# Down product: weight pairs that slide through five places, with the gate multiplied into the weight rows

## What is computed

```python
def conv_ffn(h, conv_state, w_up, w_conv, b_conv, w_down):
    ...
    a, g = jnp.split(uc, 2, axis=-1)
    out = (jax.nn.silu(a) * g) @ w_down          # (2048 x 2816) @ (2816 x 1024)
    ...
    x = x + g2 * f_out                           # g2: 1024 values, the same for every prompt token
```

## Time and profile before

| what | us |
| --- | --- |
| median of three runs | 3072.58 (3071.22 to 3073.42) |
| the profiled execution | 3067.53, its span 3065.9 |
| PE busy in the span | 2902.4 (95%) |
| DVE, ACT, POOL busy | 1959.0, 1265.5, 775.3 |
| down product, first to last matmul | 2507.2 to 3060.4 |

### The profile page before, as it was taken

How to read it: one execution, slowest core, us unless ns; L and a number is a source line. 1 busy time by engine, 2 the same in 40 slices (tenths; PEclk the granted TensorE clock), 3 DMA queues, 4 the chain that set the end, 5 groups by cost and what they waited for, 6 DMA issues and landing times.

```text
span 3065.9 us, 49134 instructions
## 1 busy us (share of the span) xinstructions
PE 2902.4 (95%) x17179; PEld 2518.6 (82%) x17179; DVE 1959.0 (64%) x2943; ACT 1265.5 (41%) x2510; POOL 775.3 (25%) x678
## 2 busy tenths in 40 slices
PE   7999999999999999999989999999999988779799
PEld 5878888887778888888879999999999976557577
DVE  2300016624988999786677777777777786676765
ACT  4611112224777887445553333334232232232322
POOL 3310003313666776120110000000000033343432
PEclk8999999999999999999999999999999999989899
DMA  6322224534422440886644444445566655535344
GB/s 215 111 77 76 74 74 153 159 123 114 125 57 58 90 95 11 304 290 197 211 170 162 155 152 154 152 148 189 179 216 210 203 182 181 193 120 198 110 151 143
DMA packets 339306, 458.54 MB, mean 150 GB/s; under 512 B 68194, under 2 KB 219944, under 8 KB 336454
## 3 DMA queue, kind: packets, MB, share of 16 engines
q1 hardware_dynamic: 325608, 415.96, 42.8%
q0 software_dynamic: 12208, 40.46, 4.0%
q10 hardware_dynamic: 1332, 0.06, 0.0%
HBM read 284.90 MB, written 171.48 MB: 149 GB/s over the span
## 4 chain that ended last, share of the span: by engine, by line
PE 44%; issue 6%; DVE 4%; POOL 3%; DMA 3%; ACT 1%; SPq 0%; DVEq 0%; POOLq 0%; ACTq 0%
PE facc L2907 29%; PE eacc L2886 6%; PE dacc L2907 4%; POOL dres L1867 2%; DMA x_d<-dres 1%; PE mpT L3056 1%; DMA dpart<-act_d 1%; PE mpm L3065 1%; PE mpS L3075 1%; PE eyT L2869 0%; POOL dT_plain L1870 0%; PE mpT L3106 0%; PE mpN L3091 0%; PE exT L2899 0%; PE mpN L3095 0%
## 5 line engine op out<-in xcount | busy, mean ns | idle before, releaser
L767 PE MATMUL pacc<-pring,h1H 128*128 128x512 f32 x1360 | 431.4, 394 | 3.4 <-ACT h1H L326 3.4
L2907 PE MATMUL facc<-fright,fsums 128*128 128x416 f32 x2112 | 418.1, 353 | 9.9 <-ACT facc L2018 6.9
L2907 PEld LDWEIGHTS facc<-fright,fsums 128*128 128x128 f32 x2112 | 398.3, 189 | 15.7 <-issue 7.5
L1183 POOL TENSOR_TENSOR aS<-aS,aC 128x512 f32<-128x512 f32 (+3 forms) x326 | 334.6, 1034 | 152.1 <-DVE aC L1123 145.7
L1123 DVE TENSOR_TENSOR_SCAN aC<-aB,aC,a 128x512 f32<-128x512 f32 (+3 forms) x326 | 362.8, 1113 | 12.1 <-ACT aB L1079 1.1
L767 PEld LDWEIGHTS pacc<-pring,h1H 128*128 128x128 f32 x1360 | 256.5, 189 | 56.4 <-ACT h1H L326 3.5
L2907 PE MATMUL facc<-fright,fwH 128*128 128x416 f32 x1056 | 290.5, 356 | 12.8 <-DVE fU L2451 11.0
L767 PE MATMUL pacc<-pring,h1L 128*128 128x512 f32 x640 | 248.0, 389 | 0.0
L1867 POOL TENSOR_TENSOR dres<-dres,dy 128x512 f32<-128x512 f32 x86 | 149.9, 1743 | 303.3 <-DVE dy L2581 234.2
L1870 POOL TENSOR_TENSOR dT_plain<-dT_plain,dB_plain 128x512 f32<-128x512 f32 x2 | 2.5, 1287 | 867.9 <-DMA db_third<-w_down 867.9
L2907 PEld LDWEIGHTS facc<-fright,fwH 128*128 128x128 f32 x1056 | 200.5, 191 | 17.7 <-issue 12.5
(11 more groups left out here) (382 smaller groups left out, 5942.4 us busy)
## 6 DMA issues: line engine op xcount, KB each, us to landing
sums_d<-fsums SPq DMA_DIRECT2D x88, 512.0 KB, 2.9
fsums<-sums_d SPq DMA_DIRECT2D x88, 512.0 KB, 4.8
fraw<-w_up SPq DMA_DIRECT2D x66, 512.0 KB, 4.1
proj_out<-pstage SPq DMA_DIRECT2D x119, 256.0 KB, 2.0
dres<-x_d SPq DMA_DIRECT2D x92, 256.0 KB, 3.3
qk_T<-pturn POOLq DMA_DIRECT2D x68, 256.0 KB, 3.1
mwa<-w_ada SPq DMA_DIRECT2D x16, 1024.0 KB, 6.6
dpart<-act_d SPq DMA_DIRECT2D x32, 512.0 KB, 4.7
```

The source lines that it names most:

```text
L767: op = mm_(acc[:, n % NB], h[:, kk, tok(t)], weight(q, w), start=(j == 0), stop=(j == len(order) - 1))
L1183: nc.gpsimd.tensor_tensor(at, at, buf[:, a + 1:b + 1], ALU.mult).then_inc(w_ready, 1)
L2907: mm = nc.tensor.matmul(bank, a[:, kk], b[:, kk], start=(begins and kk == 0 and m == 0), stop=(kk == count - 1 and m == 2), skip_group_che ...
```

## The change

Nothing ahead of the down product is changed, nor is the number of its matmuls. In it:

- **Weights slide.** There are five places for pairs. Pair 3 comes in at unit 2, pair 4 at unit 4, and so on; each stays for eight units (`STAY`). Pairs 0 and 1 leave early, at units 4 and 6, and come again at units 20 and 22. A unit works on `WINDOW[w]`: three pairs in units 0, 1 and 18 to 23, four in units 2 to 17.
- **Cells of a coming pair** are made inside the two units before it is used: its two rows are loaded (512 KB each), the sample's product runs on them at the head of the even unit, POOL multiplies them by the gate (`gate_row`), DVE makes the four sums in the even unit and the seven low halves in the odd one, ACT three of the high halves in the even unit and four in the odd one.
- **Outputs.** With the gate in the weights, DVE adds P5 to the residual (`add_five`, twice a unit) and then the bank (`add_out`, four times). `take_five`, `add_residual`, `finish_out`, `dy` and `dP` are gone.
- **Activations** come as halves into three places; the first half of unit w + 2 waits for the lefts of unit w, the second for those of w + 1.
- **First group.** POOL multiplies B11, B12 and B21 and makes T1; DVE multiplies B22 and makes T2, T4, T3 and all seven low halves.

The diff, cut:

```diff
-    GROUPS = ((0, 3), (6, 4), (14, 4))
+    NK = NF // 2
+    FIRST, ACTIVE, PLACES = 3, 4, 5
+    STAY = [(0, 4), (0, 6), (0, 8)] + [(2 * n - 4, 2 * n + 4) for n in range(FIRST, NK)] + [(20, UNITS), (22, UNITS)]
+    WINDOW = [[n for n, (a, b) in enumerate(STAY) if a <= w < b] for w in range(UNITS)]
+    COMING = {2 * v: n for v, n in enumerate([*range(FIRST, NK), None, NK, NK + 1])}
...
+            def load_act(w, e):
+                if w >= 2:
+                    sp.wait_ge(left_low, 7 if w == 2 else 7 * (w - 1 + e))
...
+            def load_rows(v):
...
+                    sp.wait_ge(*low_of("B22", COMING[2 * v - 2]))
                 for a in range(2):
+                    sp.dma_start(raw_rows[:, a], d["w_down"][(2 * kp + a) * P:(2 * kp + a + 1) * P, :]).then_inc(raw_rows_in, 16)
...
             for w in range(UNITS):
                 if w == 1:
                     store_narrow(NF - 1)
+                    sp.wait_ge(act_stored, (WIDE_STORES + NARROW_STORES) * NF)
...
+                if w + 2 < UNITS:
+                    load_act(w + 2, 0)
                 store_out(w, 0)
+                if w + 1 in COMING and w > 0:
+                    load_rows((w + 1) // 2)
                 store_out(w, 1)
...
+                if w == 1:
+                    sp.wait_ge(ends_taken, 1)
+                    for t in range(2):
+                        sp.dma_start(d["conv_out"][t], ends_t[:, t]).then_inc(ends_stored, 16)
+                    sp.wait_ge(ends_stored, 32)
+                if w + 1 < UNITS:
+                    load_res(w + 1, 2)
                 if w + 2 < UNITS:
-                    load_act(w + 2)
+                    load_act(w + 2, 1)
                 store_out(w, 3)
...
-            def add_residual(w, j):
+            def gate_row(a, n):
+                pool.wait_ge(down_gate_in, 48)
+                pool.wait_ge(raw_rows_in, 48 * event(n) + 48)
+                pool.wait_ge(sample_done, event(n) + 1)
+                nc.gpsimd.tensor_tensor(raw_rows[:, a], raw_rows[:, a], down_gate[:], ALU.mult).then_inc(cell_gated, 1)
+            def first_blocks():
...
+                for blocks_, half in ((first, 0), (b12_rows, 1), (b21_rows, 0)):
+                    for n in range(FIRST):
+                        op = nc.gpsimd.tensor_tensor(blocks_[n], blocks_[n], first_gate[half], ALU.mult)
...
-                    v.tensor_tensor(y_, down_a if j == 0 else down_b, gate_, ALU.mult).then_inc(down_gated, 1)
+            def add_five(w, j):
+                dve.wait_ge(done["P5"], UP + w + 1)
+                dve.wait_ge(res_in[j], 16 * w + 16)
+                v.tensor_tensor(res_of(w, j), res_of(w, j), down_e, ALU.add).then_inc(five_added, 1)
+            def add_out(w, j):
+                dve.wait_ge(done[("P2", "P7", "P3", "P4")[j]], UP + w + 1)
...
             def down_unit(w):
+                if w in COMING and w > 0:
+                    sample_down(w // 2)
                 for name in PRODUCTS:
...
-                        pe.wait_ge(c22_taken, UP + w + 1)
+                        pe.wait_ge(out_ready, 4 * w + 2)
```

More of the change, by code:

```diff
@@ L1954, in _ @@
             store_h2(final)
[L1955 to L1959 removed]
+            first_blocks()
+            for n in COMING.values():
+                if n is not None:
+                    gate_row(0, n)
+                    gate_row(1, n)
         @block.scalar
@@ L2169, in down_slot @@
+                if w % 2 and coming is not None:
+                    for name in HIGHS[1][3:]:
+                        cell_high_of(name, coming)
                 down_seed_b(w)
-                if changed:
-                    cell_high_of("T3", g)
-                take_five(w)
-                if change:
-                    cell_high_of("B11", g + 1)
-                down_seed_c(w)
-                if changed:
-                    cell_high_of("B22", g)
-                if w + 1 == UNITS:
-                    return
@@ L2569, in cell_low_of, with first_low_of @@
+            def first_low_of(name):
+                dve.wait_ge(cell_high, HIGHS[0].index(name) + 1)
+                dve.wait_ge(cell_sum, {"T1": 1, "T2": 2, "B22": 3}.get(name, 0)) if name in ("T1", "T2", "B22") else None
+                if name == "B11":
+                    dve.wait_ge(cell_sum_pool, 1)
+                top, low, own = first_cells(name)
+                if name == "B21":
+                    for n in range(FIRST):
                         op = v.tensor_tensor(low[:, n], b21_rows[n], top[:, n].bitcast(F32), ALU.subtract)
@@ L3033, in down_unit @@
                     else:
-                        pe.wait_ge(c22_taken, UP + w + 1)
-                    three(banks[name], left(one, w)[0:2], cell(other, g)[0:2], name in ("P1", "P5"), done[name])
+                        pe.wait_ge(out_ready, 4 * w + 2)
+                    high, low, _ = left(one, w)
+                    for i, n in enumerate(WINDOW[w]):
+                        b_high, b_low_, _ = cell(other, n)
+                        for m, (a, b) in enumerate(((high, b_high), (high, b_low_), (low, b_high))):
+                            mm = nc.tensor.matmul(banks[name], a[:, i], b, start=(name in ("P1", "P5") and i == 0 and m == 0),
+                                                  stop=(i == len(WINDOW[w]) - 1 and m == 2), skip_group_check=True)
+                    mm.then_inc(done[name], 1)
+                    if (w, name) == (0, "P7"):
+                        sample_down(0)
                     if (w, name) == (1, "P2"):
```

529 lines of the change are left out of this document (245 added, 284 removed).

## The result

The changed kernel takes 3034.5 us (median of four runs, 3032.8 to 3039.4), the kernel before 3072.1 us beside it: ratio 0.988, 95% interval 0.9863 to 0.9897. So 37.6 us less, where 64.2 were forecast.

The account below looks back on a forecast made before the run. TensorE needs 441 of the down product's 553.2 us; 112 are idle time and half clock. Unit times summed to 489.7 (-63.5), with -0.7 at the end: 3072.6 - 64.2 = 3008.4 us; range 2980 to 3040, likeliest case 2994 to 3030.

Parts of the forecast that it names:

- the holes at units 8 and 16: TensorE stops of about 15 us at each of two weight-group changes, caused on VectorE and GpSimd; forecast to go.
- The loop: Activation load waits behind residual load, which waits for output 2's store; 41.2 us per pair of four-pair units bringing new pairs.
- Rival 2: Loop longer: 22.5 us for each of 18 units, waits adding up to 0.1 us per operation; 3049 us; chance 0.13.
- Three-pair units: Units 18 to 23: the loop gives 18.2 and 18.8 us, 74.0 for units 18 to 21; then 15.9 and 14.8.
- The entry: Units 0 and 1: VectorE gets 18.6 us more work, loses meetings with GpSimd; TensorE +7, so 54.6 us.
- GpSimd's part in the even units: Two 1024-column multiplications of 2.5 us each run while VectorE waits for activations, so they cost nothing.
- GpSimd's first blocks: Entry: twelve 512-column operations, about 16 us, hidden behind the up product; counted at 0, with 6 us kept.
- The new rows: New pair's rows land in about 5 us; TensorE waits about 1 us (0 to 3) at unit heads, seven times.
- Rival 3: Slower: GpSimd's lock costs 5 us plus 2.5 us of clock per gated pair, 11 at entry; 3095 us; chance 0.09.
- Rival 1: The loop hides: half loads land in 3.3 us, rows never late, entry +4; 2986 us; chance 0.13.
- the list of signs: No hole over 5 us; units 2 to 17 at 19.6 to 21.5, 18 to 21 at 17.5 to 19.5; GpSimd operation near 2.5.

Follow-up runs that it names:

- x1: Changed kernel with the load of the activations' second half put ahead of the residual load in SP's queue: 3015.5 us, ratio 0.9818.
- x2: Changed kernel with the activations' second half loaded, from unit 2 on, once VectorE's sum S4 is done, ahead of store 2: 3010.9 us, ratio 0.9798.
- x7: Changed kernel with GpSimd's gate multiplication of each coming weight row cut to 2 columns from 1024: 3029.6 us, ratio 0.9853.
- x4: Changed kernel with GpSimd's first gate waiting for output 2 of unit 0, and ScalarE's unit 1 copy of bank a to b before four T cells: 3031.0 us.
- x11: x9 with ScalarE's copy of bank b to c in unit 1 also moved before the four high halves of T blocks: 3000.1 us, ratio 0.9772.
- x8: Changed kernel with GpSimd's gate multiplications of the first blocks cut to 2 columns from 512: 3034.6 us, ratio 0.9873.
- y2: Kernel before, with GpSimd's additions of the residual cut to 2 columns from 512: 3045.7 us, ratio 0.9917.
- y1: Kernel before, keeping its three groups, with VectorE adding P5 and banks into the residual, no gate, no ScalarE copy of P5 or GpSimd additions: 3042.3 us, ratio 0.9897.
- x9: Changed kernel with the edits of x4 and x2, and output 1 ahead of the coming pair's last sums and low half on VectorE: 2999.8 us, ratio 0.9766.
- x3: Changed kernel with ScalarE copying bank b to c between the high halves of A11 and S1: 3039.6 us, ratio 0.9895.

## Why the prediction was right, and where it was not

**The total.** The down product came out 33.5 us over its forecast (523.2 for 489.7), which is over half of the gain that was forecast. That the total stayed in the range is in part luck: it owes as much to the range's width of 60 us as to the sum. What the prediction had right is the mechanism: the holes at units 8 and 16 go, and a loop through store and load takes part of it back (x1, x2).

**The loop** was named right, with its place and its path. Its size was off mostly in one term, the load: "4.0, since it travels alone". It did not travel alone. The residual load into place 2 was issued just ahead of it and store 3 0.4 us behind. From the first low half in unit 8 (2711.36) to that in unit 9 (2733.77) are 22.4 us: 13.2 for VectorE's 19 operations (forecast 12.8), 2.9 from the issue of the store to that of the load (2.6), 5.6 from there to ScalarE (4.0), 0.7 for ScalarE's copy (0.6). Over the fourteen such loads of units 3 to 16 it is 5.2 us on average (4.75 to 6.0) from issue to ScalarE. What makes one longer than another no run here separates: in unit 10 the load has the same neighbours in the queue and takes 4.75. The issue table of the last two visits, from issue to landing, gives 4.7, the upper bound that the earlier trace rows showed before:

```profile
dres<-x_d SPq DMA_DIRECT2D x63, 256.0 KB, 3.5
dpart<-act_d SPq DMA_DIRECT2D x17, 512.0 KB, 4.7
...
draw_rows<-w_down SPq DMA_DIRECT2D x12, 512.0 KB, 4.4
```

Rival 2, the longer loop, had 22.5 us a unit; 22.1 is the mean over units 2 to 15. So these units lie near rival 2's figure and not at the forecast's 20.7, and the whole, between the two, is nearer to rival 2 (3049) than to the forecast. But rival 2's reason is not what happened: it put a tenth of a microsecond on each operation, and the 19 operations took 0.4 us more than counted; it is the load again.

The terms as written do not quite give the sum either. What follows output 2 (2.1, 0.4, 0.1, 4.0 and 0.6) is 7.2 us and not 7.3 to 7.5, and with two pauses of 0.70 the three-pair units would be 18.7 and 19.3, not 18.2 and 18.8.

**Three-pair units** have the same cause in the main, 80.2 for 74.0; without the loop they take 71.5 (x2). In unit 21 the load reached ScalarE 5.3 us after its issue at 2983.49 and TensorE stood before P7:

```profile
2983.49 0.85 SPq L1654 DMA_DIRECT2D dpart<-act_d  x2
...
2988.76 0.52 ACT L1975 ACTIVATE dA<-dpart 128x384 fp32r<-128x384 f32 x1 [6.02 <-DMA dpart<-act_d]
...
2992.73 1.52 PE L3049 MATMUL dacc<-dT_fifth,dS 128*128 128x512 f32 x3 [4.72 <-ACT dacc L1975]
```

**The entry**, 61.9 for 54.6, of which 1.9 are the head of unit 2, failed in two steps. It had VectorE's added work, but not that GpSimd's first gate, released by the sample's product in unit 0, would meet the convolution: 4.9 us (x7), by two operations that were stretched, one in each row of 3.34 us (the expectations of x4 and x7 read each row as one operation). "GpSimd's part in the even units" spoke of units 2 and up only. Nor had it ScalarE's copy in unit 1 behind four cells that are not summed yet; x4 and x11 show that without it VectorE would hold TensorE a little later. GpSimd's first blocks were counted at nothing, with 6 us kept: nothing is what they cost (x8).

**The new rows** cost less than the 1 us at each of seven unit heads: they landed in 4.4 us (counted: about 5), and for unit 10 they were issued at 2741.69, and the sample's product starts at 2747.55 without a wait of its own.

**The source of the gain** was wrong. The prediction took the holes at units 8 and 16 as the price of the change of group, and said of GpSimd's additions that nobody on the path waited for them long. That is true of waits, and it was the wrong question: nearly nothing waits for them by a semaphore, but VectorE's operations are longer beside them (y2, -26.0). Most of the gain came without the slide in y1 (-30.5), which has no gate at all; what a place for the gate would cost there was not run. The slide is what removes the holes, which y1 keeps, and without its loop it is worth at least as much as the chain (some 36 us, x2). The prediction also took TensorE for full in visits two and three outside the changes. In the kernel before, units 11 to 15 take 13.7 us more than five times 19.53, and units 2 to 6 of the first visit 32.7 more than five times 14.8, the sample's products included.

**Rival 3** (GpSimd's lock, slower) fell: x7 prices all ten coming pairs at 4.9 us together. **Rival 1** (the loop hides, 2986) is what x9 comes near to, within 14 us, with the early load and the edits at entry and outputs. Of the list of signs: no hole over 5 us at units 8 and 16 held; GpSimd's operation of 1024 columns took 2.4; 19.6 to 21.5 us held for the even units and not for the odd ones; 17.5 to 19.5 held for units 18 and 20 (19.0 and 18.3) and not for 19 and 21.

## What to carry to other kernels

When a load is moved behind another in a queue, write down what the one ahead waits for; here a store of 2.5 us and a load beside it closed a loop that held most of 18 units and took 24 us of the gain. Ask of an operation on GpSimd not only who waits for it but what VectorE does meanwhile, and put it into VectorE's pauses; the busy time of VectorE at the same number of operations shows the price. A wait that goes away when one engine's order is changed proves nothing until the next wait of the same unit is read (x3, x11).

## What the runs showed of the chip

In these traces a VectorE operation that reads a bank (facc, dacc) keeps its length beside GpSimd, one that reads two buffers outside the banks does not. In the changed kernel its 68 additions of bank dacc (durations in ns: minimum, median, maximum) all keep their length, some of them beside GpSimd, as at 2704.92:

```profile
L2588 DVE TENSOR_TENSOR dres<-dres,dacc x68: 678/680/690, 2540.6 to 3033.1; 128x512 f32<-128x512 f32 x68
```

And in y1 three additions of facc from 2674.92 on run at 0.6 us each within GpSimd's 4.95 us, while the subtraction in front of them, two buffers, had taken 4.98. In y2, the addition that reads a bank and the multiplication by the gate that reads two buffers (times in ns: minimum, median, maximum):

```profile
L2585 DVE TENSOR_TENSOR dy<-dacc,dP x44: 676/684/693, 2566.9 to 3033.8; 128x512 f32<-128x512 f32 x44
L2587 DVE TENSOR_TENSOR dy<-dy,dgate x44: 691/692/4474, 2567.6 to 3034.5; 128x512 f32<-128x512 f32 x44
```

The Trainium skill has this as a rule (SBUF — State Buffer, Who interferes with whom): an instruction with at most one input in that buffer, outside the modes that use both ports, does not contend with GpSimd. The traces agree, with these numbers. It is one more thing that the new chain has over the old: its additions all read a bank, and two of the old four outputs needed a step that did not (44 of these, 775 ns on average in the kernel before, so it is worth little there).

How long TensorE had waited did not alone say whether its clock fell. In x11, nine us apart, and behind them a row of x2:

```profile
2534.58 2.32 PE L3060 MATMUL dacc<-dT,dA 128*128 128x512 f32 x9 [2.51 <-DVE dres L2599]
...
2543.69 4.18 PE L3060 MATMUL dacc<-dT,dS 128*128 128x512 f32 x9 [2.59 <-ACT dacc L1981]
```

```profile
2589.66 4.58 PE L3053 MATMUL dacc<-dT,dA 128*128 128x512 f32 x12 [1.92 <-DVE dres L2592]
```

After 2.51 us nine passes went at the level of 2.4 GHz (granted clock 1.00), after 2.59 us at that of 1.2 (0.50). In x2 a wait of only 1.92 us was followed by twelve passes in 4.58 us and not 2.96 (granted clock 0.50 from 2590 to 2593). The three waits of 6.3 to 7.3 us in the changed kernel's entry were followed by 3.75 to 4.18 us for nine passes.
